# 512-column products in the dense feed-forward, and unread matmuls in the rwkv, attention and norm stages

## The reference, cut to what matters

```python
for i in range(2):                       # block 1
    z = rms_norm(h, g_mix[i]) @ w_in[i]  # three mixers share one projection
    y = concat(spatial_gating(z_a), rwkv7_time_mix(z_b), nsa_attention(z_c))
    h = h + y @ w_out[i]
    hn = rms_norm(h, g_ffn[i])           # layer 0: dense, layer 1: 8 experts
    h = h + ((silu(hn @ w1) * (hn @ w3)) @ w2 if i == 0 else moe_swiglu(hn))
    h = h + (p[i] @ ple_proj_w[i]) * sigmoid(rms_norm(h, g_ple[i]) @ ple_gate_w[i])
x = rms_norm(h, g_final)
for l in range(2):                       # block 2
    x = x + 0.5 * swiglu(rms_norm(x, g0), ffn[l, 0])
    h = rms_norm(x, g1); proj = h @ w_in[l]
    ya, yb, yc = neighbourhood(proj), differential(proj), window_gqa(proj)
    x = x + (sum of sigmoid(h @ w_gate[l] + b)[b] * (y_b @ w_branch[l, b])) @ w_o[l]
    x = x + 0.5 * swiglu(rms_norm(x, g2), ffn[l, 1])
out = rms_norm(x, final_g)
```

## Time and profile before

| | us |
|---|---|
| median of three runs | 3417.7 |
| lowest and highest | 3416.36, 3421.22 |
| the profiled execution, as timed | 3421.73 |
| its span in the profile | 3419.6 |
| mean granted clock | 0.895 |

### The profile page before, as it was taken

The page is one execution under the profiler, slowest core; times in us unless marked ns, Lnnn a source line. Parts: engine busy times, 40 slices in busy tenths (PEclk is TensorE's granted clock), DMA queues, the critical chain, the costliest instruction groups (busy, mean ns, idle before and its releaser), DMA issues. The chain is left out here.

```text
span 3419.6 us, 48764 instructions
## 1 busy us (share of the span) xinstructions
PE 3058.7 (89%) x19310; PEld 2680.6 (78%) x19310; DVE 1989.5 (58%) x2765; ACT 1550.8 (45%) x2285; POOL 0.2 (0%) x4
## 2 busy tenths in 40 slices
PE   6798899789879999999999799959899898869898
PEld 5695798778567777877777798938899898849897
DVE  4426454343539888898887355476355555475354
ACT  3213333321328777777776333345333434354333
POOL 0000000000000000000000000000000000000000
PEclk9755999875589999999999899979999999979999
DMA  6300354410028888889887454604455455316451
GB/s 246 118 1 25 125 187 145 140 47 1 1 117 309 325 321 341 320 323 355 320 321 285 150 186 159 190 21 148 148 192 187 156 187 176 106 37 205 142 187 58
DMA packets 106548, 599.07 MB, mean 175 GB/s; under 512 B 25012, under 2 KB 33546, under 8 KB 37528
## 3 DMA queue, kind: packets, MB, share of 16 engines
q1 hardware_dynamic: 99144, 590.97, 46.7%
q10 hardware_dynamic: 7248, 5.88, 0.6%
HBM read 593.91 MB, written 6.12 MB: 175 GB/s over the span
## 5 line engine op out<-in xcount | busy, mean ns | idle before, releaser
L2130 DVE TENSOR_TENSOR expert_w_low<-weight_ring,expert_w_high 128x1024 fp32r<-128x1024 f32 x528 | 629.5, 1223 | 75.4 <-ACT expert_w_high L2077 64.8
L2077 ACT ACTIVATE expert_w_high<-weight_ring 128x1024 fp32r<-128x1024 f32 x528 | 552.5, 1058 | 95.8 <-PE psum L2006 54.0
L619 PE MATMUL psum<-hnT_high,weight_high 128*128 128x256 f32 x1760 | 503.4, 286 | 22.4 <-DVE weight_low L665 22.4
L619 PE MATMUL psum<-hnT_low,weight_high 128*128 128x256 f32 x1760 | 503.0, 286 | 0.0
L619 PE MATMUL psum<-hnT_high,weight_low 128*128 128x256 f32 x1760 | 502.7, 286 | 0.0
L665 DVE TENSOR_TENSOR weight_low<-weight_ring,weight_high 128x1024 fp32r<-128x1024 f32 x330 | 391.6, 1220 | 19.0 <-ACT weight_high L659 18.5
L659 ACT ACTIVATE weight_high<-weight_ring 128x1024 fp32r<-128x1024 f32 x330 | 335.2, 1054 | 67.9 <-PE psum L631 61.8
L619 PEld LDWEIGHTS psum<-hnT_high,weight_high 128*128 128x128 f32 x1760 | 342.8, 195 | 28.1 <-DVE weight_low L665 24.2
L619 PEld LDWEIGHTS psum<-hnT_low,weight_high 128*128 128x128 f32 x1760 | 342.8, 195 | 3.9
L619 PEld LDWEIGHTS psum<-hnT_high,weight_low 128*128 128x128 f32 x1760 | 342.6, 195 | 0.0
L516 DVE TENSOR_TENSOR slab_low<-weight_ring,slab_high 128x2048 fp32r<-128x2048 f32 (+3 forms) x120 | 205.4, 1725 | 210.4 <-ACT slab_high L508 210.4
(11 more groups left out here) (395 smaller groups left out, 5457.3 us busy)
## 6 DMA issues: line engine op xcount, KB each, us to landing
weight_ring<-in_moe_w SPq DMA_DIRECT2D x264, 1024.0 KB, 6.9
weight_ring<-in_w_in SPq DMA_DIRECT2D x52, 1024.0 KB, 6.8
weight_ring<-in_ffn_w_gate SPq DMA_DIRECT2D x44, 1024.0 KB, 4.9
weight_ring<-in_ffn_w_up SPq DMA_DIRECT2D x44, 1024.0 KB, 6.8
weight_ring<-in_ffn_w_down SPq DMA_DIRECT2D x44, 1024.0 KB, 4.9
weight_ring<-in_ffn_w SPq DMA_DIRECT2D x33, 1024.0 KB, 5.0
weight_ring<-in_w_gate SPq DMA_DIRECT2D x24, 1024.0 KB, 4.9
weight_ring<-in_w_branch SPq DMA_DIRECT2D x24, 512.0 KB, 3.5
```

The costliest lines, as they stand in the source:

```text
L619: last = nc.tensor.matmul(K.bank[4 + t % 3][:, k * SEQ:(k + 1) * SEQ], w[:, kt, :], x[:, kt, :], start=(j == 0), stop=(j == len(steps) - 1))
L2077: nc.scalar.activation(part(0, k, half), raw(c, k, half), ACT.Copy).then_inc(high[k].sem, 1)
L2130: nc.vector.tensor_tensor(part(1, k, half), raw(c, k, half), as_f(part(0, k, half)), ALU.subtract).then_inc(low[k].sem, 1)
```

## The change

Four parts.

1. **Dense feed-forward.** The high and low parts of the activations lie side by side in one tensor (hn_parts returns both views and the whole). For each slice the high weights multiply both parts in one product of 512 columns, and the low weights multiply the high part in one of 256. So the sums of k = 0 and k = 1 fill a bank each, in banks 4 and 5 or 6 and 7 in turn, and their two halves still have to be added: VectorE does so with two reductions (gate_sum, lift). ScalarE's silu waits for the first and reads SBUF; tile_up(t) waits for hidden tile t - 2.
2. **Unread matmuls** (keep_busy): n products of float32r, 128x128 weights, as many columns as the output given, 512 or 128, into a bank that nobody reads. 12 at the start of each norm and 2 before its third pair of turned blocks; 14 at the end of rwkv_inputs; in each level of rwkv_invert one behind each half of NX, one in the middle and one at the end of each half of XNX; in rwkv_recur 5 of 128 columns before the wait for the right-hand side and 8 before the wait for U; in each step of attention_stage 2 behind the scores and 1 behind the turn.
3. **Room for them.** Attention's values use bank 6 alone, so values(g) waits for the stored values of g - 1. The squares in rwkv_recur share Z's buffer. Constants that block 1 alone uses move to a tensor of their own; the others stay.
4. **Setup** loads the constants in two DMAs and copies the two operands of keep_busy on VectorE.

```diff
+    def keep_busy(self, n, out):
+        for _ in range(n):
+            self.nc.tensor.matmul(out, self.busy_w[:, :], self.busy_x[:, 0:out.shape[-1]], start=True, stop=True,
+                                  skip_group_check=True)
...
+                nc.vector.tensor_copy(K.busy_w[:, :], K.c("ident"))
+                nc.vector.tensor_copy(K.busy_x[:, :].rearrange("p (a b) -> p a b", b=P), K.c("upto").unsqueeze(1).broadcast_to([P, 4, P]))
...
             def _(t):
+                K.keep_busy(12, K.bank[7][:, :])
                 for b in range(4):
+                    if b == 2:
+                        K.keep_busy(2, K.bank[7][:, :])
...
+            def sums(t, k):
+                return K.bank[4 + 2 * (t % 2) + k]
+
             def tile_up(t, i=None):
-                if i is not None or t >= 3:
-
-                    wait(nc.tensor, hid, t - 2, TB, i)
+                if i is not None or t >= 2:
+
+                    wait(nc.tensor, hid, t - 1, TB, i)
...
-                    steps = [(w, x, kt) for kt in range(KT) for w, x in ((hi, hn[0]), (hi, hn[1]), (lo, hn[0]))]
-                    for j, (w, x, kt) in enumerate(steps):
-                        last = nc.tensor.matmul(K.bank[4 + t % 3][:, k * SEQ:(k + 1) * SEQ], w[:, kt, :],
-                                                x[:, kt, :], start=(j == 0), stop=(j == len(steps) - 1))
+                    out = sums(t, k)
+                    for kt in range(KT):
+                        nc.tensor.matmul(out, hi[:, kt, :], hn[2][:, kt, :, :], start=(kt == 0), stop=(kt == KT - 1),
+                                         skip_group_check=True)
+                        last = nc.tensor.matmul(out[:, 0:SEQ], lo[:, kt, :], hn[0][:, kt, :], start=False, stop=(kt == KT - 1),
+                                                skip_group_check=True)
...
-                    wait(nc.scalar, up, t + 1, TB, i)
-                    nc.scalar.activation(gate[:, t % 3, :], K.bank[4 + t % 3][:, 0:SEQ], ACT.Silu).then_inc(silu.sem, 1)
+                    wait(nc.scalar, K.gate_summed, t + 1, TB, i)
+                    nc.scalar.activation(gate[:, t % 3, :], gate_sum[:, t % 3, :], ACT.Silu).then_inc(silu.sem, 1)
...
+                    wait(nc.vector, up, t + 1, TB, i)
+                    halves = lambda k: sums(t, k).rearrange("p (a b) -> p b a", a=2)
+                    nc.vector.tensor_reduce(gate_sum[:, at, :], halves(0), AX.X, ALU.add).then_inc(K.gate_summed.sem, 1)
+                    nc.vector.tensor_reduce(lift[:, at, :], halves(1), AX.X, ALU.add).then_inc(K.lift_summed.sem, 1)
...
                 last.then_inc(*pe.mark("g"))
+                K.keep_busy(14, K.bank[7][:, :])
...
                         last.then_inc(*pe.mark(("NX", i, b)))
+                        K.keep_busy(1, K.bank[7][:, :])
...
                             last = nc.tensor.matmul(at_m(4, m), NX[:, m, :], XT[:, m, :], start=True, stop=True)
+                            if m % 8 == 3:
+                                K.keep_busy(1, K.bank[7][:, :])
                         last.then_inc(*pe.mark(("XNX", i, b)))
+                        K.keep_busy(1, K.bank[7][:, :])
...
+                spare = K.bank[4][:, 0:P]
...
+                    K.keep_busy(5, spare)
                     t.wait_ge(*dve(("rhs", c)))
...
                     last.then_inc(*pe.mark(("U", c)))
+                    K.keep_busy(8, spare)
                     t.wait_ge(*act(("U", c)))
...
-                    if g >= 2:
-                        t.wait_ge(*ou(g - 1))
+                    if g >= 1:
+                        t.wait_ge(*ou(g))
...
                         scores(s)
+                    K.keep_busy(2, K.bank[7][:, :])
                     if 0 <= s - LEAD < U:
                         turn(s - LEAD)
+                    K.keep_busy(1, K.bank[7][:, :])
```

More of the change, by code:

```diff
@@ L154, in shape_constants @@
     return {name: np.asarray(v, np.float32) for name, v in c.items()}
+KEPT = ("ident", "ones", "na_mask", "window")
 CONST_AT = {}
-for _name, _v in shape_constants().items():
+for _name, _v in sorted(shape_constants().items(), key=lambda item: item[0] not in KEPT):
     CONST_AT[_name] = (sum(w for _, _, w in CONST_AT.values()), _v.shape[0], _v.shape[1])
 CONST_W = sum(w for _, _, w in CONST_AT.values())
+KEPT_W = sum(CONST_AT[_name][2] for _name in KEPT)
 class WeightRing:
@@ L307, in setup_stage @@
         dve = Steps(K.dve_step, ["zeroed", "bias"])
-        total = len(VEC1) + len(VEC2) + 3
+        total = len(VEC1) + len(VEC2) + 4
         def load_vectors(eng, rows, vec):
@@ L558, in dense_ffn_stage @@
     with ctx:
-        gate = K.tmp(ctx, "gate_act", [P, 3, SEQ])
+        gate, gate_sum, lift = (K.tmp(ctx, n, [P, 3, SEQ]) for n in ("gate_act", "gate_sum", "lift"))
         hidden = K.tmp(ctx, "hidden", [P, 3, SEQ])
@@ L694, in tile @@
                 def tile(t, i=None):
+                    at = t % 3
+                    wait(nc.vector, up, t + 1, TB, i)
+                    halves = lambda k: sums(t, k).rearrange("p (a b) -> p b a", a=2)
+                    nc.vector.tensor_reduce(gate_sum[:, at, :], halves(0), AX.X, ALU.add).then_inc(K.gate_summed.sem, 1)
+                    nc.vector.tensor_reduce(lift[:, at, :], halves(1), AX.X, ALU.add).then_inc(K.lift_summed.sem, 1)
                     wait(nc.vector, silu, t + 1, TB, i)
-                    at = t % 3
-                    nc.vector.tensor_tensor(hidden[:, at, :], gate[:, at, :], K.bank[4 + at][:, SEQ:2 * SEQ], ALU.mult)
-                    nc.vector.tensor_tensor(hid_hi[:, at, :], gate[:, at, :], K.bank[4 + at][:, SEQ:2 * SEQ],
+                    wait(nc.vector, K.lift_summed, t + 1, TB, i)
+                    nc.vector.tensor_tensor(hidden[:, at, :], gate[:, at, :], lift[:, at, :], ALU.mult)
+                    nc.vector.tensor_tensor(hid_hi[:, at, :], gate[:, at, :], lift[:, at, :],
                                             ALU.mult).then_inc(K.hid_high.sem, 1)
@@ L975, in _ @@
                         tokens = slice(None) if left == "w" else slice(left * P, (left + 1) * P)
-                        steps = [([part[:, kt, cols] for part in w], [x[:, kt, tokens] for x in hn]) for kt in range(KT)]
+                        steps = [([part[:, kt, cols] for part in w], [x[:, kt, tokens] for x in hn[0:2]]) for kt in range(KT)]
                         last = product3(nc, out, steps if left == "w" else [(x, y) for y, x in steps], ready)
@@ L1375, in rwkv_recur @@
         rhs, U = sb("solve_rhs", [RC, RH, HD]), sb("U", [RC, 2, SEQ])
-        Y, sq, bv, Z = (sb(n, [RC, NM, HD]) for n in ("Y", "Y_sq", "bonus_v", "Z"))
+        Y, bv, Z = (sb(n, [RC, NM, HD]) for n in ("Y", "bonus_v", "Z"))
+        sq = Z
         stat = sb("gn_stat", [RC, 3, NM])
@@ L1597, in values @@
                             wide = v.shape[-1]
-                            out = K.bank[6 + g % 2][j * HD:j * HD + wide, 0:P]
+                            out = K.bank[6][j * HD:j * HD + wide, 0:P]
                             last = nc.tensor.matmul(out, v, turned_at(u, j, kb, probT), start=(n == 0), stop=(n == len(terms) - 1))
@@ L1681, in store_values @@
                     a.wait_ge(*pv(g + 1))
-                    nc.scalar.activation(groups[g][1], K.bank[6 + g % 2][:, 0:P], ACT.Copy).then_inc(ou.sem, 1)
+                    nc.scalar.activation(groups[g][1], K.bank[6][:, 0:P], ACT.Copy).then_inc(ou.sem, 1)
                 for s in range(U + LEAD + 2):
@@ L2335, in _ @@
                     for j in range(tiles):
-                        steps = [([part[:, kt, j * P:(j + 1) * P] for part in w], [x[:, kt, :] for x in hn]) for kt in range(KT)]
+                        steps = [([part[:, kt, j * P:(j + 1) * P] for part in w], [x[:, kt, :] for x in hn[0:2]]) for kt in range(KT)]
                         last = product3(nc, bank[:, j * SEQ:(j + 1) * SEQ], steps, ready)
@@ L2341, in _ @@
                         for b in range(NBLK):
-                            steps = [([x[:, kt, b * P:(b + 1) * P] for x in hn], [part[:, kt, tiles * P:256] for part in w])
+                            steps = [([x[:, kt, b * P:(b + 1) * P] for x in hn[0:2]], [part[:, kt, tiles * P:256] for part in w])
                                      for kt in range(KT)]
@@ L2543, in _ @@
                         w, bank = S.both(2 * n + k), K.bank[3 * k + n % 3]
-                        left = [of(part, n % 3) for part in y_parts] if k else hn
+                        left = [of(part, n % 3) for part in y_parts] if k else hn[0:2]
                         for j in range(2):
@@ L2674, in hn_parts @@
 def hn_parts(K, ctx):
-    return [K.tmp(ctx, name, [P, KT, SEQ], F32R) for name in ("hnT_high", "hnT_low")]
+    both = K.tmp(ctx, "hnT_parts", [P, KT, 2, SEQ], F32R)
+    return both[:, :, 0, :], both[:, :, 1, :], both
 def block1(K, tensors, arg):
+    K.const1 = K.tmp(tensors, "shape_consts1", [P, CONST_W - KEPT_W])
     T = Block1Tensors(K, tensors)
```

13 lines of the change are left out of this document (9 added, 4 removed).

## The result

The changed kernel takes 3484.7 us (median of 4 runs, 3480.45 to 3486.21), the kernel before 3417.03 (4 runs, 3411.88 to 3421.22) beside it: ratio 1.019, 95% interval 1.0178 to 1.0202. The prediction was 3461 us, between 3400 and 3490, slower with a chance of 0.72. The profiled executions, on which all that follows rests, span 3419.6 and 3477.0 us, 57.4 apart.

The account below looks back on a forecast made before the run. TensorE, busy 89% of the span, was taken to set the pace nearly everywhere. Terms -22 + 50 - 1 + 13 - 2 + 9 - 4 = +43 us on 3417.7 gave 3461 us, range 3400 to 3490.

Parts of the forecast that it names:

- Inversion: 64x64 matrix inversion, both layers: clock stays at 0.50, six unread products a level add 0.70 us each, +50 us.
- Feed-forward: Five dense feed-forward stages: paired products cut a slice from 0.360 to 0.347 us, -22 us (-24 to -15).
- The cover: Dense feed-forward: hidden tile ready after about 2.8 us, within 5.5 us of TensorE's next up product; VectorE not the bound.
- Recurrence: rwkv recurrence, both layers: unread products overrun the waits by 0.55 and 1.26 us per chunk, +13 us (10 to 15).
- Attention of block 2: Six block 2 attentions: 0.68 us of unread products a unit, partly visible, plus cold starts, +9 us (-3 to +25).
- The single bank of the values: Attention values: one bank instead of two adds a wait for ScalarE's copy of the group before, costing nothing.
- Sparse attention: Block 1 sparse attention, two stages: clock rises in the first few units and stays, -2 us (-14 to +12).
- Norms: Twelve norms: unread products fit TensorE's wait, transposes may run faster, -4 us (-14 to +6).
- the warm starts: Products behind the norms: mostly start as cold as now, one in five starts warm at -2.3 us.
- The 14 products behind the gate matrix: End of rwkv inputs: too early to help the inversion, cost nothing, transposes may run warm, -1 us for both layers.
- Rival (a): rwkv stages: full-size products lift the clock, decided at the inversion's first level, -60 us, 3358 us; chance 0.17.
- The argument against it: Inversion: full-size products are one in seventeen records and start from the low level, so the clock would not rise.

Follow-up runs that it names:

- experiment 8: Changed kernel with the six unread products of each inversion level given 64x64 weights, the neighbours' form, still 512 columns: 3478.94 us, ratio 1.017.
- experiment 2: Changed kernel with no unread product anywhere; paired feed-forward products, smaller constants and single bank of the values stay: 3408.26 us, ratio 0.9964.
- experiment 7: Changed kernel plus 16 unread products ahead of each inversion, six per level kept, none in the recurrence and attentions: 3393.6 us, ratio 0.9915.
- experiment 9: Changed kernel with 16 unread products ahead of each inversion, two per level, none in the recurrence and attentions: 3365.83 us, ratio 0.9832.
- experiment 12: Changed kernel with six unread products ahead of each inversion, two per level, none in the recurrence and attentions: 3359.26 us, ratio 0.9819.
- experiment 3: Changed kernel plus 16 unread products ahead of the first level of each inversion, the six per level kept: 3409.47 us, ratio 0.9971.
- experiment 5: Changed kernel plus 16 unread products ahead of each inversion, four per level instead of six (those of XNX): 3395.87 us, ratio 0.9927.
- experiment 6: Changed kernel plus 16 unread products ahead of each inversion, two per level (end of each half of XNX): 3382.28 us, ratio 0.9887.
- experiment 10: Changed kernel with the six unread products of each inversion level in one run behind XNX, nothing added at entry: 3393.97 us, ratio 0.9911.
- experiment 4: Changed kernel with 16 unread products ahead of the first level of each inversion and none within the levels: 3412.25 us, ratio 0.9975.

## Why the prediction came out as it did

The direction, the place and the clock were right: the inversion stayed at 0.50, was full, and all six products of a level were added to its time. The size was short by 24 us of medians (3461 against 3484.7), or by 14 of the 57.4 us between the two profiled executions. The terms missed by 33 us, all in one direction, and stages without a term of their own gave 18 back, 8.6 of them the first projection: without that luck the forecast would have been further off. By the terms of the sum:

- **Inversion, +50 forecast, +64 measured.** The mis-sized term. 0.70 us was the columns plus 0.27 for two changes of form, read off. It was 0.89, and the reason given was mostly wrong: the change of form makes at most 0.11 of the 0.46 us above the columns (experiment 8), the rest comes with a lone product of this type also in its neighbours' form. The earlier trace rows has one step from float32r to float32, with a change of form: 117.03 to 117.33, 0.30 us where 0.213 is the pace. It has none the other way, and no such product alone between float32 ones.
- **Feed-forward, -22 forecast, -11.5 measured.** The pitch of a slice was expected at 0.347. From the timeline of the changed kernel, the first and the last of sixteen slices:

```profile
504.09 0.39 PE L641 MATMUL psum<-hnT_parts,weight_high 128*128 128x512 f32 x1
504.32 0.28 PE L643 MATMUL psum<-hnT_parts,weight_low 128*128 128x256 f32 x1
504.43 0.40 PE L641 MATMUL psum<-hnT_parts,weight_high 128*128 128x512 f32 x1
...
509.38 0.40 PE L641 MATMUL psum<-hnT_parts,weight_high 128*128 128x512 f32 x1
```

  5.29 us / 15 = 0.353: the 512-column product takes 0.23 to 0.24 when one of 256 follows, against the 0.227 of neighbours of one size, and half of a saving of 0.013 was gone. 0.007 x 352 = 2.5 us a stage, where the stages show 1.8 to 3.4, 2.3 in the mean. The cover held: TensorE's one wait in the stage is for its first weights, and VectorE is busy 130 of 188 us. Its reductions, by line:

```profile
L723 DVE TENSOR_REDUCE gate_sum<-psum 128x256 f32<-128x512 f32 x110 | 76.1, 691 | 256.9 <-PE psum L643 256.9
```

  691 ns against the 686 taken from the earlier trace rows.
- **Recurrence, +13 forecast, +14.4 measured.** The timeline of one chunk, to be held against the earlier trace rows:

```profile
270.68 0.68 PE L1442 MATMUL psum<-state,hnT 64*64 64x64 f32 x7
271.29 1.33 PE L254 MATMUL psum<-busy_x,busy_w 128*128 128x128 f32 x5
272.54 1.11 PE L1450 MATMUL psum<-solve_rhs,XT 64*64 64x64 f32 x8
273.59 1.97 PE L254 MATMUL psum<-busy_x,busy_w 128*128 128x128 f32 x8
275.48 0.49 PE L1458 MATMUL psum<-U,zb 64*64 64x64 f32 x4
```

  From the state products to U's 1.86 us (1.27 before), from U's to the next 2.94 (1.57): 0.59 and 1.37 late, forecast 0.55 and 1.26. Experiments 2 and 7 confirm it by taking them out.
- **Attention of block 2, +9 forecast, +9.8 measured, but not for the reason given alone.** In the four kernels without unread products there (experiments 2, 7, 9 and 12) the six stages still take 152.7 to 155.5 us in sum against 150.7 before. So 2 to 5 us belong to something else in the change, and the unread products bear the other 5 to 8. The single bank of the values, which the prediction had costed at nothing, is the only edit left in these stages, and the trace shows its wait. Who TensorE waits for in the first attention of block 2 (us in total, times, longest), in the kernel before and in experiment 2 (its first 22 us):

```profile
PE psum L1599 <- ACT probT L1678: 0.8, 4, 0.2
```

```profile
PE psum L1638 <- ACT branchT L1723: 1.6, 4, 0.5
```

  Before, the values wait for the turned map (probT); in experiment 2 they wait for ScalarE to store the values of the group before (branchT), in all six stages 9.0 us. TensorE's holes in these stages rise from 32.0 to 36.6 us. The bank was not tried alone, and the clock is low for other parts of these stages in each execution, so its price is known only as 2 to 5 us. In return the merges behind the attentions are 3.0 us shorter in the changed kernel; they are not in experiment 2.
- **Sparse attention, -2 forecast, +2.5 measured.** The clock rose from 0.64 to 0.93 as expected, and TensorE is busy 64.6 of 65.4 us instead of 59 of 65: the products took what the clock gave. Without them the stages take 63.9 to 66.9 us, the same, at 0.66 in the first one of experiment 2.
- **Norms, -4 forecast, -3.3 measured**: -0.4 to -0.8 in ten of them, +0.4 and +1.8 in two. The -4 is about what the norms alone come to by the prediction's figures (8 x -0.8 and 4 x 0.5); the warm starts that it names, one in five at -2.3, are not in it, and these products did not bring them: the feed-forward gain is the same with and without (experiment 2), and the choice of the experts, 2.0 us shorter, is 2.3 shorter in experiment 2.
- **The 14 products behind the gate matrix, -1 forecast, 0 measured.** In the changed kernel's profile the stage behind them lasts 18.1 us as before, but in six of the eleven other kernels that have them it lasts 13.6 in the first layer, never in the second, and the clock is up in it. In experiment 2, which has none of them, it lasts 18.1. So they seem to be worth 4.6 us in some executions and nothing in others; one profile without them is too few to say that it never lasts 13.6 then.
- **The first projection, no term, -8.6 measured** between the two profiled executions, as told above.

Rival (a) had the mechanism half right. "It decides at the point where the mixed stream is taken as activity": entered at the high level it holds (experiments 3, 5, 6), as spread in this change it does not raise. The argument against it, one in seventeen records and a low start, was true for this layout and no more: the same six in a run raise it (experiment 10). The Trainium skill, "TensorE: Matmul & The Clock Gate", Part 1, has sustained activity release the throttle. Here the same count of products released it together and did not apart, while TensorE was busy for 91.0 of 93.7 us with them apart: this trace disagrees with it if busy time is taken for activity.

## What to carry to other kernels

Where a stage of small products runs at the lower clock, don't sprinkle full-size products over it: put a short run of them (six of 512 columns, 2.9 us) in front, where the engine waits anyway, and then only as many as hold the level (two in a level of 6.8 us did). A shorter run, and fewer than two a level, were not tried. Read the granted clock of the stage first, for at the lower level a lone product cost 0.89 us here and at the higher 0.57. Where a latency chain sets the pace, as in the recurrence, leave them out.

## What had not been expected of the hardware

- Raising and holding differ. A stream of 64x64 float32 products, busy but for one hole of 0.44 us, ran at 1.00 until 169.5 us and, without any hole, at 0.50 from 170.5 us to the end (experiment 4); two 128x128 products of 512 columns in each level kept it at 1.00 for 41 us (experiment 6). The six of a level did not raise it one by one in 93.7 us, and did in one run of 2.85 us (experiment 10).
- A float32r product alone between float32 products costs some 0.46 us above its columns at the lower clock, and mostly not because of the tile's form (0.78 us in all with the neighbours' form, 0.89 without); six in a run start 0.475 us apart on average.
- Columns are not all of a product's pace: 512 columns took 0.227 us among their like and some 0.233 ahead of a product of 256 (0.353 a slice less 0.12).
